# A fused encoder layer on one core: a different order of high and low products, matmuls on zeros, a re-cut parameter computation and a re-arranged second LayerNorm

## The reference

```python
proj = x @ w_in                       # 2048 x 8192: q, k, v, u (1024 each), g_att, g_ssm (2048 each)
y_att = neighbourhood_attention(q, k, v, rpb) @ w_na_out       # 8 heads of 128
y_s = gelu(s5_forward(u) + s5_backward(u) + d * u)             # 64 groups, 64 complex states each
y_s = y_s * sigmoid(y_s @ w_glu + b_glu)
y_ssm = y_s @ w_s5_out
mix = (sigmoid(g_att + b) * y_att + sigmoid(g_ssm + b) * y_ssm) @ w_out
h = layer_norm(alpha * x + mix, ln1_g, ln1_b)
ff = (silu(h @ w_ffn_gate) * (h @ w_ffn_up)) @ w_ffn_down      # inner width 5632
out = layer_norm(alpha * h + ff, ln2_g, ln2_b)
```

## Time and profile before

| | |
|---|---|
| median of 3 runs | 1439.03 us (1438.48 to 1439.33) |
| profiled execution | 1439.54 us, of which its span (first to last instruction) is 1437.5 us |
| TensorE busy | 1398.9 us, 97% of the span |
| VectorE, ScalarE, POOL busy | 955.7, 722.1, 219.2 us |
| HBM read | 260.19 MB, 185 GB/s over the span |
| LayerNorm 1, last matmul before to first turn after | 669.44 to 674.25 us |
| LayerNorm 2, last matmul to last vector instruction | 1419.14 to 1434.78 us |

### The profile page before, as it was taken

One profiled execution on the slowest core, in us unless ns is written; L12 is line 12 of the kernel. 1 busy time (PEld: TensorE's weight loads), 2 busy tenths in 40 slices (PEclk: granted clock), 3 DMA queues, 4 the chain that ended last, 5 costly groups with the idle time before them and its releaser, 6 DMA issues.

```text
span 1437.5 us, 23329 instructions
## 1 busy us (share of the span) xinstructions
PE 1398.9 (97%) x8928; PEld 1199.2 (83%) x8928; DVE 955.7 (66%) x1217; ACT 722.1 (50%) x1026; POOL 219.2 (15%) x182
## 2 busy tenths in 40 slices
PE   7899999999999999998999999999999999999995
PEld 6777888888888888887888888888888888888884
DVE  7969888898876679756655555555555554545546
ACT  5353665556654885434644444444445443333332
POOL 2694323443200000000021111000000000000002
PEclk9999999999999999998999999999999999999998
DMA  8665555555555667664556556655765566666662
GB/s 281 192 208 147 180 170 172 157 161 178 164 159 156 188 227 259 186 198 131 184 180 189 188 181 188 188 182 186 245 187 183 185 189 192 191 196 195 193 193 86
DMA packets 87835, 266.38 MB, mean 185 GB/s; under 512 B 13776, under 2 KB 22096, under 8 KB 87248
## 3 DMA queue, kind: packets, MB, share of 16 engines
q1 hardware_dynamic: 84224, 261.96, 58.9%
q10 hardware_dynamic: 3536, 3.38, 0.7%
HBM read 260.19 MB, written 5.11 MB: 185 GB/s over the span
## 4 chain that ended last, share of the span: by engine, by line
PE 91%; DVE 7%; DMA 1%; SPq 0%; ACT 0%; issue 0%; DVEq 0%; ACTq 0%
PE bank L1502 40%; PE bank L1503 20%; PE bank L1515 8%; PE bank L1517 8%; PE bank L1516 8%; DVE wlo L943 2%; PE bank L1583 2%; PE bank L1552 1%; PE bank L1604 1%; DMA raw<-wstream 1%; PE bank L1565 1%; DVE scratch L969 1%; PE bank L1630 0%; PE bank L1614 0%; DVE scratch L966 0%; DVE hp L1347 0%
## 5 line engine op out<-in xcount | busy, mean ns | idle before, releaser
L1502 PE MATMUL bank<-act,whi 128*128 128x512 f32 x2304 | 824.5, 402 | 11.3 <-DVE wlo L947 7.1
L943 DVE TENSOR_TENSOR wlo<-raw,whi 128x1024 fp32r<-128x1024 f32 x463 | 584.5, 1265 | 358.2 <-ACT whi L534 354.4
L534 ACT ACTIVATE whi<-raw 128x1024 fp32r<-128x1024 f32 x463 | 489.5, 1058 | 455.2 <-PE bank L1503 233.8
L1503 PE MATMUL bank<-act,wlo 128*128 128x256 f32 x2304 | 647.0, 281 | 0.0
L1502 PEld LDWEIGHTS bank<-act,whi 128*128 128x128 f32 x2304 | 434.6, 189 | 118.5 <-DVE wlo L947 7.1
L1503 PEld LDWEIGHTS bank<-act,wlo 128*128 128x128 f32 x2304 | 436.8, 190 | 0.2
L1515 PE MATMUL bank<-whi,mid 128*128 128x512 f32 x352 | 136.9, 389 | 0.0
L1516 PE MATMUL bank<-wlo,mid 128*128 128x512 f32 x352 | 136.9, 389 | 0.0
L1517 PE MATMUL bank<-whi,mid 128*128 128x512 f32 x352 | 136.9, 389 | 0.0
L522 POOL TENSOR_TENSOR hp<-hp,lnrow 128x512 f32<-128x512 f32 x3 | 5.0, 1664 | 544.9 <-ACT hp L935 544.9
L1515 PE MATMUL bank<-whi,act 128*128 128x512 f32 x192 | 75.8, 395 | 4.1 <-DVE wlo L943 4.1
(11 more groups left out here) (161 smaller groups left out, 1318.8 us busy)
## 6 DMA issues: line engine op xcount, KB each, us to landing
raw<-wstream SPq DMA_DIRECT2D x463, 512.0 KB, 3.7
lnrow<-lnrows SPq DMA_DIRECT2D x4, 1024.0 KB, 6.3
xraw<-xT SPq DMA_DIRECT2D x8, 256.0 KB, 6.6
bcn<-bc_rows SPq DMA_DIRECT2D x8, 256.0 KB, 4.4
bm<-bias SPq DMA_DIRECT2D x8, 256.0 KB, 4.1
tb<-lag_dram SPq DMA_DIRECT2D x32, 64.0 KB, 3.6
hp<-xtok SPq DMA_DIRECT2D x4, 512.0 KB, 4.8
out<-hp SPq DMA_DIRECT2D x8, 256.0 KB, 2.3
```

The source lines that it names most:

```text
L534: act.activation(whi[:, c % SPL, :], raw[:, c % RAW, :], ACT.Copy).then_inc(hi_ready, 1)
L943: dve.tensor_tensor(wlo[:, c % SPL, :], raw[:, c % RAW, :], whi[:, c % SPL, :].bitcast(F32), ALU.subtract).then_inc(lo_ready, 1)
L1502: pe.matmul(bank[:, :], hi, both, start=start and i == 0, stop=stop and i == kn - 1)
L1503: mm = pe.matmul(bank[:, 0:T], lo, act[:, k0 + i, 0, :], start=False, stop=stop and i == kn - 1, skip_group_check=True)
```

## The change

1. In `prod_w` the eight high products of a tile come first, then its eight low products.
2. `keep_busy` issues float32 matmuls of 256 columns on a zeroed tile `S`: 7 before the first product, 9 before the first `h_rows`.
3. The parameter computation is cut into other pieces and spread over tiles 0 and 3 to 20. `form_b(0)` moves from POOL to VectorE (`form_b0`, behind tiles 21 and 22); `form_c(0)` moves to tiles 23 and 25.
4. `v_last` moves from VectorE to ScalarE.
5. LayerNorm 2: VectorE multiplies six blocks by the gain during the down stage (`times_gain`). Behind the last matmul the two row halves get their statistics one after the other. TensorE turns the column (shift, 1) into two rows and makes shift*gain + bias for each of six blocks with a matmul on two partitions; VectorE then needs one instruction per block. ScalarE and POOL take blocks 3 and 7. The rows `lnrow` are loaded in three transfers.

```diff
-LN2_DVE, LN2_POOL = [0, 1, 2, 4, 5], [3, 6, 7]
-LN2_STORES = [0, 3, 1, 2, 6, 4, 7, 5]
+LN2_DVE, LN2_POOL = [0, 1, 2, 4, 5, 6], [3, 7]
+LN2_BANKS = (0, 1, 2, 3, 6, 7)
+LN2_STORES = [0, 3, 1, 2, 7, 4, 5, 6]
...
-            for r in range(2):
-                sp.dma_start(lnrow[:, r, :], lnrows[2 + r:3 + r, :].to_broadcast([P, D])).then_inc(ln2_landed, 16)
+            sp.dma_start(lnrow[:, 0, :], lnrows[2:3, :].to_broadcast([P, D])).then_inc(ln2_landed, 16)
+            sp.dma_start(lnrow[:, 1, 1536:D], lnrows[3:4, 1536:D].to_broadcast([P, 512])).then_inc(ln2_landed, 16)
+            sp.dma_start(lnrow[0:2, 1, 0:1536], lnrows[2:4, 0:1536]).then_inc(ln2_landed, 16)
...
-            form_b(0)
             a_rows()
...
+                        if j == 1:
+                            act.wait_ge(w_used, H_V + 16)
+                            act.wait_ge(v_stored[0], 16)
+                            for t in range(TT):
+                                act.activation(vout[:, t, :], ps[bank_of(N_V + 2 + t)][:, :], ACT.Copy).then_inc(uv_copied, 1)
...
-            sd(1)
-            act.wait_ge(ln_step, 4)
-            for i in LN2_POOL:
-                t = i // 4
-                v = hp[:, t, i % 4 * 512:i % 4 * 512 + 512]
-                act.activation(v, v, ACT.Identity, scale=lnm[:, t, 2:3], bias=lnm[:, t, 3:4]).then_inc(ln2_norm, 1)
+            load_sqrt(1)
+            act.wait_ge(ln_step, 2)
+            for t in range(TT):
+                act.wait_ge(var_ready, 3 + t)
+                act.activation(lnm[:, t, 4:5], lnm[:, t, 1:2], ACT.Sqrt, bias=eps1[:, :]).then_inc(sd_ready, 1)
+                act.wait_ge(ln_step, 4 + 2 * t)
+                v = hp[:, t, 1536:D]
+                act.activation(v, v, ACT.Identity, scale=lnm[:, t, 2:3], bias=lnm[:, t, 6:7]).then_inc(ln2_norm, 1)
+                act.wait_ge(ln2_turned, t + 1)
+                act.activation(mrow[0:2, t, :], ps[4][0:2, t * P:(t + 1) * P], ACT.Copy).then_inc(mrow_ready, 1)
...
+            def form_b0(r):
...
+                if r == 0:
+                    dve.wait_ge(bc_staged[0], 16)
+                    dve.tensor_tensor(wide(lo), br, kr, ALU.mult).then_inc(bp_prod, 1)
+                    dve.tensor_tensor(wide(hi), bi, ki, ALU.mult).then_inc(bp_prod, 1)
+                    dve.wait_ge(bp_prod, 2)
+                    dve.tensor_tensor(lo, lo, hi, ALU.add).then_inc(b_formed, 1)
...
             def parameters(j):
...
                 if j == 3:
-                    time_steps(0)
+                    exp_poly(0)
+                    exp_poly(1)
                 elif j == 4:
-                    time_steps(1)
-                elif j == 6:
-                    decays(0)
-                elif j == 7:
-                    decays(1)
+                    exp_out(None, DT)
+                    tt(X, ARE, DT, ALU.mult)
+                    tt(Y, AIM, DT, ALU.mult)
+                elif j == 5:
+                    reduce_exp(X)
+                elif j in (6, 7):
+                    exp_poly(j - 6)
+                elif j == 8:
+                    exp_out(EM, EX)
                 elif j == 9:
+                    angles()
+                elif j == 10:
                     sines()
                 elif j == 11:
                     cosines()
-                elif j in (12, 13):
-                    gains(j - 12)
-                elif j in (14, 15, 16, 17):
-                    powers(j - 14)
-
+                elif j == 12:
+                    whole_angles()
+                elif j in (13, 14):
+                    gains(j - 13)
+                elif j in (15, 16):
+                    powers(j - 15)
+                elif j in (18, 19, 20):
+                    powers(j - 16)
+
+            dve.memset(S[:, :, :], 0.0).then_inc(warm_ready, 1)
...
+                    if i == 0:
+                        dve.wait_ge(par_landed, 16)
+                        reduce_exp(DT)
...
-            dn_evac(3)
-            dve.wait_ge(ln2_landed, 32)
-            moments(1, lambda: centre(LN2_DVE[0]))
+                if c == 26:
+                    dve.wait_ge(ln2_landed, 48)
+                if c >= 26 and (c - 26) % 22 < 2:
+                    times_gain((c - 26) % 22, (c - 26) // 22)
+            residual(N_DN + 6, H_DN + 87, 0, 3)
+            variance(0)
+            residual(N_DN + 7, H_DN + 87, 1, 3)
+            scale_shift(0)
+            variance(1)
+            scale_shift(1)
             for n, i in enumerate(LN2_DVE):
-                if n > 0:
-                    centre(i)
                 t, b = i // 4, slice(i % 4 * 512, i % 4 * 512 + 512)
-                dve.wait_ge(ln2_gain, n + 1)
-                dve.scalar_tensor_tensor(out=hp[:, t, b], in0=hp[:, t, b], scalar=lnm[:, t, 2:3], in1=lnrow[:, 1, b],
-                                         op0=ALU.mult, op1=ALU.add).then_inc(ln2_dve, 1)
+                dve.wait_ge(ln2_row, n + 1)
+                dve.wait_ge(ln2_gain, 6)
+                dve.scalar_tensor_tensor(out=hp[:, t, b], in0=hp[:, t, b], scalar=lnm[:, t, 2:3],
+                                         in1=ps[LN2_BANKS[n]][:, :], op0=ALU.mult, op1=ALU.add).then_inc(ln2_dve, 1)
...
-                    hi, lo = (w[:, s, i * P:(i + 1) * P] for w in (whi, wlo))
                     both = act[:, k0 + i, :, :].rearrange("p h n -> p (h n)")
-                    pe.matmul(bank[:, :], hi, both, start=start and i == 0, stop=stop and i == kn - 1)
-                    mm = pe.matmul(bank[:, 0:T], lo, act[:, k0 + i, 0, :], start=False, stop=stop and i == kn - 1,
-                                   skip_group_check=True)
+                    pe.matmul(bank[:, :], whi[:, s, i * P:(i + 1) * P], both, start=start and i == 0, stop=stop and i == kn - 1)
+                for i in range(kn):
+                    mm = pe.matmul(bank[:, 0:T], wlo[:, s, i * P:(i + 1) * P], act[:, k0 + i, 0, :], start=False,
+                                   stop=stop and i == kn - 1, skip_group_check=True)
                 mm.then_inc(w_used, 1)
...
+            def keep_busy(bank, count):
+
+                for i in range(count):
+                    pe.matmul(bank[:, 0:T], S[:, 0, 0:P], S[:, 0, :], start=True, stop=True)
+
+            pe.wait_ge(warm_ready, 1)
+            keep_busy(ps[7], 7)
...
+            pe.wait_ge(res_added, 6)
+            keep_busy(ps[0], 9)
...
+            def turn_shift(t):
+
+                pe.wait_ge(ln_step, 4 + 2 * t)
+                pe.transpose(ps[4][0:2, t * P:(t + 1) * P], lnm[:, t, 6:8], ident[:, :]).then_inc(ln2_turned, 1)
...
+            turn_shift(0)
+            for n, i in enumerate(LN2_DVE):
+                t, b = i // 4, slice(i % 4 * 512, i % 4 * 512 + 512)
+                if n == 2:
+                    turn_shift(1)
+                pe.wait_ge(mrow_ready, t + 1)
+                pe.matmul(ps[LN2_BANKS[n]][:, :], mrow[0:2, t, :], lnrow[0:2, 1, b], start=True, stop=True).then_inc(ln2_row, 1)
```

129 lines of the change are left out of this document (69 added, 60 removed).

## The result

The kernel after takes 1427.76 us (median of 4 runs, 1427.68 to 1427.98), the kernel before beside it 1438.76; the ratio is 0.9924, with a 95% interval of 0.9911 to 0.9937. It is faster by 11.0 us where 23.7 were forecast: the direction was right and the time lies inside the stated range, but the gain is less than half of the forecast.

What follows compares the result with a forecast made beforehand. TensorE, busy 97% of the span, was taken as the bound: its stream plus the gaps outside it. Terms 12.7 + 0.6 + 0.4 + 4.7 + 1.5 + 4.0 = 23.9 us gave 1415.1 us; own range 1409 to 1421, with rivals 1402 to 1430.

Steps and rivals of the forecast that it cites:

- the first rival: Product order in `prod_w`: low products no faster in a row, 126.7 ns, order worth 0; 1428 us; chance 0.16.
- the second rival: Low products in `prod_w` run at the rate of weight loads, 108 to 109 ns; 1385 us; chance 0.12.
- the fourth: Low products in a row wait for their weights, 190 ns each: +157 us over 312 tiles; chance 0.05.
- The third: `form_b0` makes VectorE the bound at 1.59 us per operation, turning +4.7 into -3: 1423 us; chance 0.05.
- the low products' 120 ns: Grouped tiles of `prod_w`: a low product behind a low one was taken to cost 120 ns, bounds 108 and 126.7.
- the zeros at LayerNorm 1: Nine matmuls on zeros before the first turn keep the full clock, so the second tile begins earlier: 0.4 us.
- Part 1: High products first in `prod_w`: 53 ns less per tile, 11.4 us over 216 tiles plus 1.3 in the head loop: 12.7 us.
- tiles already at 346.7 gain nothing: `prod_w` tiles whose high and low pair already takes the faster 346.7 ns were priced at no gain from grouping.
- Parts 2 and 3 at the start: Start, u and v: zeros gain 0.6 us at tile 3, finer parameter pieces 4.7 us; 5.3 us in all.
- 5.9 - 1.2 = 4.7: u and v: TensorE's 5.9 us of losses to VectorE go, less 1.2 us of backlog from `form_b0` at tile 21.
- Part 4: Head loop: `v_last` on ScalarE removes TensorE's 1.4 us wait plus restart, 1.5 us; 0 without ScalarE's slack.
- Part 5: LayerNorm 2 behind the last matmul: 5.6 us gain at full clock, 0.5 at half throughout; the middle taken, 4.0 us.

Runs made afterwards that it cites:

- only_order: The kernel before with only the new loop, eight high products of a tile first and then its eight low ones: 1433.08 us, ratio 0.9973.
- alt_order: The kernel after with the old loop of `prod_w` back, each low product right behind its high one: 1434.03 us, ratio 0.9953.
- no_early_piece: The kernel after with the parameter piece of tile 0, between the first two pairs of x, moved behind tile 3: 1427.01 us, ratio 0.9928.
- tail_zeros: The kernel after with six more matmuls on zeros behind the last product, five before the first turn and one behind it: 1425.98 us, ratio 0.9921.
- pool_after: The kernel after with GpSimd's clearing of its buffers held back until VectorE has done the early parameter piece: 1426.06 us, ratio 0.9924.
- pool_cold: The kernel after with GpSimd's clearing held back and without the matmuls on zeros at the start: 1426.86 us, ratio 0.9927.
- c_at_24: The kernel after with the second half of forming C behind tile 24 instead of 25: 1427.15 us, ratio 0.9921.
- best: The kernel after with products two and two, 128-partition row matmuls and zeros in the tail, GpSimd's clearing held back, C behind tiles 23 and 24: 1418.77 us, ratio 0.9868.
- tail_full: The kernel after with six matmuls on zeros behind the last product and row matmuls on 128 partitions instead of 2: 1424.61 us, ratio 0.9898.
- pairs_tail: The kernel after with products two high and two low by turns, zeros in the tail and row matmuls on 128 partitions: 1421.50 us, ratio 0.9888.
- order_mix: The kernel after with another product order in each stage, among them two and two, four and four, one and one: 1433.44 us (one execution).

## Why the prediction was right and wrong

The time, 1427.8, is that of the first rival (1428), but not by its mechanism: it had low products no faster in a row and the order worth nothing, and the order is worth 6 us with low behind low at 120 ns. That the time came out there is chance: four terms missed, not one. That pitch also puts out the second rival (108) and the fourth (190). The third had VectorE's operations for B at 1.59; the trace has them at 0.69 to 0.84, and part 3 comes to nothing for other reasons.

What the forecast had right: that the time is TensorE's stream plus the gaps; that no part does harm as a whole; the low products' 120 ns; the zeros at LayerNorm 1 (0.4 forecast; 504.74 with them and 505.11 without, in the new order, 0.37; 0.70 in the old one). These are single executions, and in three others with the zeros the stage was 1.2 to 2.0 us longer, so the last agrees by luck as much as by reason.

One sum of the prediction is wrong beside its argument. With the figures that it takes from the Trainium skill's formula (TensorE: Matmul & The Clock Gate, section Back-to-back issue gap), 109 and 216 ns, part 1 would come to some 67 us (an estimate) and not 45: 8 x (353.3 - 325) ns in 240 tiles and 8 x (346.7 - 325) in 72. The section gives this formula for a single matmul's gap and says that in a stream with its own loads both set the distance, so it was no rule for this stream; the distances here are 120 and 226.7.

The 23.9 us missed the 11.6 of the profiles in four terms:

- **Part 1, forecast 12.7, measured 6.1 in the stages behind v** (1.33 + 5.45 + 0.04 - 0.71; 5.6 and 6.3 us in the times of only_order and alt_order). The step that failed is the price of a tile, 8 x (226.6 + 120.1) = 2774 ns: the 226.6 came from a long run of one width and the 120 was estimated for one, and both are right for such runs (226.7 and 120), but a tile of two widths has a change in it, and "only neighbours change" put its cost at nothing. It is 19 ns a tile (2793 against 2774), 27 more on the high side and 8 less on the low, 4.1 us over 216 tiles. The second step that failed is "tiles already at 346.7 gain nothing": they lose 2.4 ns a pair. In the head loop, where 72 of 96 tiles were of that kind by the prediction's own count, each of the six middle heads takes 44.99 us in only_order instead of 44.87, and the loop has -0.7 where 1.3 was counted. The last 0.5 fits the low products that stand last in the fed tile, which the prediction had counted under LayerNorm 1 and which two and two win back. The premise was also thinner than I put it: 353.3 is no fixed price of the old order. The old order can run at 346.7 in the same stages, and did so in gate and up in about one execution in nine of the kernel before, going by their times. At that pace it beats the grouping by 4 us (1423.7 against 1427.8). What the grouping brings is that this isn't drawn: no execution of a grouped kernel lies 8 to 10 us from the others, and all 10 of only_order lie within 1.6 us. Smaller differences stay (3.6 us in no_early_piece, 3.2 in tail_zeros).
- **Parts 2 and 3 at the start, forecast 5.3, measured 0.0 over u and v.** "5.9 - 1.2 = 4.7" took the waits as gone but for B. The finer pieces did shorten u's stalls, but the piece put between the pairs of x wasn't priced at all, with the x pair behind it and GpSimd beside it: that it met GpSimd's clearing cost 1.7 us (pool_after; 2.2 by the stages), in which the zeros' share (about 1, pool_cold) was lost too. And C's second half, moved to tile 25, brought the wait that the forecast had only for B: 0.9 us of v (c_at_24). With both mended, best has 107.39 where the kernel before has 110.97: 3.6 us, of which the order in pairs has a share.
- **Part 4, forecast 1.5, measured 3.2.** The mechanism was right and the size off. I read one wait (1.4) from the earlier trace rows, whose window ends at 130 us, before the third of the three stalls that the same copy caused (1.39, 0.32 and 1.36 us); the second I counted to u and v.
- **Part 5, forecast 4.0, measured 1.9.** "I take the middle" between a clock that holds and one that falls. It fell at 1414 and did not come back under the row matmuls on two partitions, of which tail_zeros shows that the clock falls under them even where TensorE never stands. The bounds that were written down, 0.5 for half clock throughout and 5.6 at full clock, are near what was seen (0.3 in alt_order, 6.0 in tail_full); the middle was the wrong choice (0.3 to 2.2 over ten profiles). What the Trainium skill says of turns could not be told apart here, since the clock fell under row matmuls.

Most of the shortfall could be won back: mending the start, C, the tail and the order within a tile gave back 9.0 us, and 1418.8 stands 3.7 above the forecast's 1415.1. What remains open is what draws the pace of alternation, and why the changes of width cost what they do. Over the 2774 ns of the two long-run paces a tile takes 19 ns more with one change from low to high (eight and eight), 33 with two (four and four), 13 with four (two and two), and none or 53 with eight (alternation). The records show where the time goes, not why; neither order nor stage alone decides it.

## What to carry to other kernels

A price borrowed from another stage must come from the same mix of neighbours, and an average over a group hides what its edges cost: four orders of the same sixteen matmuls cost 346.7 to 353.4 ns a pair, and over 216 tiles that is more than the rest of this change. Work put in front of a fed stream is priced by what stands behind it in its queue and by who runs beside it, not by its own length. And where a tail depends on the clock, look in a trace at the granted clock under the very matmuls that it has before counting on it.

## What the hardware showed unexpectedly

- Alternating 512- and 256-column products run at 353.4 or at 346.7 ns a pair, the same instructions in the same stage, and it differs from one execution to the next: 7 of 65 executions of the kernel before are 8 to 10 us quicker, about the 9.3 us that 176 tiles at 53 ns make. Grouping by eight (349.1) or two (348.4) gives one pace in all profiles taken.
- In a group of eight 512-column products behind narrow ones the first five distances are 232 ns on average and the last three 226.7; in the eight 256-column ones behind them the first is 113 and the others 119 to 120. So the price of a product depends on neighbours up to five back.
- TensorE busy without a gap on matmuls with two partitions goes to 1.2 GHz (granted 0.51 from 1416); with 128 partitions at the same place and with the same columns it stays at 2.4 (1.00) until they are done, in all three profiles (tail_full, pairs_tail, best).
- Of 14 profiles of kernels with the zeros at LayerNorm 1 the clock held in the fed tile behind it in seven and fell in seven; in three of these the stage was 1.2 to 2.0 us longer, in three no longer, and order_mix can't be compared. A stage comparison across two single profiles has that error.
- A `TENSOR_SCALAR` of 128 x 64 (0.19 us alone) took 0.7 to 2.0 us beside GpSimd's clearing of a buffer, where a subtraction with two inputs ran at its usual 0.69.
